# A hybrid attention/GLA/MoE layer on one core: the first two projections in quarters, shift and scale 256 columns at a time

## The reference

```
sh1, sc1, g1, sh2, sc2, g2 = split(SiLU(cond) @ w_ada + b_ada, 6)   # 1024 -> 6 x 1024
h = LN(x) * (1 + sc1) + sh1
q_a, k_a, v_a, q_g, k_g, v_g, r_g, lr, mg = split(h @ w_in)
```

## Time and profile before

| | |
|---|---|
| median of 3 runs | 675.63 us (674.58 to 676.66) |
| profiled execution: time, span | 672.36 us, 670.6 us |
| PE busy | 621.0 us, 93% |
| DVE, ACT, POOL busy | 40%, 16%, 17% |
| chain that ended last | PE 60%, DMA 22%, DVE 8% |

### The profile page before, as it was taken

One profiled execution on the slowest core, in us unless ns is written; L12 is line 12 of the kernel. 1 busy time (PEld: TensorE's weight loads), 2 busy tenths in 40 slices (PEclk: granted clock), 3 DMA queues, 4 the chain that ended last, 5 costly groups with the idle time before them and its releaser, 6 DMA issues.

```text
span 670.6 us, 8592 instructions
## 1 busy us (share of the span) xinstructions
PE 621.0 (93%) x3403; PEld 344.4 (51%) x3403; DVE 265.9 (40%) x593; ACT 106.6 (16%) x222; POOL 115.6 (17%) x114
## 2 busy tenths in 40 slices
PE   6999999999999999999999998999999887788994
PEld 3553355546455556555544464665566544444541
DVE  4322533145445544302224865334333232222347
ACT  2001553110032222330000021111111111111000
POOL 4000000010300000000001323334334222221102
PEclk9999999999999999999999999999999999988998
DMA  9998737344131130409995097899999999999862
GB/s 336 376 332 289 251 127 251 126 158 157 24 127 58 69 126 1 126 0 317 372 402 223 38 359 296 333 420 416 413 414 417 413 417 414 415 416 419 352 241 94
DMA packets 56200, 176.65 MB, mean 263 GB/s; under 512 B 10644, under 2 KB 12724, under 8 KB 44512
## 3 DMA queue, kind: packets, MB, share of 16 engines
q1 hardware_dynamic: 39264, 143.34, 55.4%
q10 hardware_dynamic: 11152, 24.47, 10.4%
q0 software_dynamic: 5744, 8.28, 3.5%
HBM read 174.58 MB, written 11.96 MB: 278 GB/s over the span
## 4 chain that ended last, share of the span: by engine, by line
PE 60%; DMA 22%; DVE 8%; issue 2%; POOL 2%; ACT 2%; SPq 2%; ACTq 0%; DVEq 0%; POOLq 0%
PE bank L1592 13%; PE bank L1865 11%; DMA X<-exp_w_up 8%; PE bank L1581 7%; PE bank L1766 6%; PE bank L1874 5%; DMA Y<-exp_w_up 4%; PE bank L1545 3%; DMA Y<-ln_b 3%; DMA X<-w_ada 2%; PE bank L1505 2%; DMA Y<-w_ada 2%; POOL rstd L689 2%; PE bank L1839 2%; PE bank L1733 1%
## 5 line engine op out<-in xcount | busy, mean ns | idle before, releaser
L1865 PE MATMUL bank<-X,Y 128*64 128x256 f32 x672 | 82.0, 395 | 11.8 <-DMA X<-exp_w_up 10.8
L1592 PE MATMUL bank<-Y,W 128*128 128x384 f32 x256 | 86.6, 492 | 0.0
L1865 PEld LDWEIGHTS bank<-X,Y 128*64 128x64 f32 x672 | 50.7, 137 | 48.0 <-DMA X<-exp_w_up 18.0
L689 POOL TENSOR_TENSOR rstd<-ss,cst 128x1 f32<-128x1 f32 (+3 forms) x21 | 22.6, 1075 | 295.7 <-DVE ss L822 295.7
L1592 PEld LDWEIGHTS bank<-Y,W 128*128 128x128 f32 x256 | 47.4, 190 | 36.0 <-issue 5.6
L1581 PE MATMUL bank<-W,Y 128*128 128x512 f32 x144 | 64.0, 597 | 0.0
L732 POOL DMA_INDIRECT Y<-h_rows,gidx x32 | 41.4, 1293 | 92.9 <-PE bank L1839 88.4
L1192 DVE COPY abias<-bank 128x128 f32<-128x128 f32 x32 | 9.3, 292 | 117.1 <-PE bank L1898 117.1
L1865 PE MATMUL bank<-W,Y 128*64 128x256 f32 (+1 forms) x320 | 37.2, 346 | 7.5 <-DMA W<-exp_w_up 3.9
L737 POOL DMA_INDIRECT pair_rows<-PTr,sidx x32 | 32.9, 1029 | 61.2 <-DVE PTr L1206 60.6
L1779 PE MATMUL bank<-X,Y 128*128 128x512 f32 x96 | 41.7, 594 | 1.3 <-issue 1.0
(11 more groups left out here) (232 smaller groups left out, 723.2 us busy)
## 6 DMA issues: line engine op xcount, KB each, us to landing
X<-exp_w_gate SPq DMA_DIRECT2D x22, 1024.0 KB, 22.1
X<-exp_w_up SPq DMA_DIRECT2D x22, 1024.0 KB, 26.1
X<-exp_w_down SPq DMA_DIRECT2D x22, 1024.0 KB, 26.6
Y<-w_ada ACTq DMA_DIRECT2D x16, 1024.0 KB, 8.2
W<-w_in SPq DMA_DIRECT2D x7, 2048.0 KB, 9.0
W<-exp_w_gate SPq DMA_DIRECT2D x10, 1024.0 KB, 22.1
W<-exp_w_up SPq DMA_DIRECT2D x5, 1024.0 KB, 26.7
W<-exp_w_down SPq DMA_DIRECT2D x5, 1024.0 KB, 29.7
```

Source lines behind the costliest of these rows:

```text
L689: nc.gpsimd.tensor_tensor(rstd[:, 0:n], ss[:, 0:n], const("mhalf", 0, n), ALU.pow)\
L1592: ins = mm(bank[:, 0:TOKENS], w[:, k, c * P:(c + 1) * P], hT[:, :, k, :], start=k == 0, stop=k == KT - 1)
L1865: ins = mm(bank[hh * 64:hh * 64 + 64, a:b], x_[:, c, h * 64:h * 64 + 64], rhs(hh), start=k == 0 and a == 0, stop=k == KT - 1, skip_group_c ...
```

## The change

The constants are loaded in two parts: `ident` and `selcol` first, the rest after the second quarter. The -0.5 that GpSimd takes a power with is a memset of its own. Shift and scale are computed in four steps of 256 columns each (`shift_scale(g)`: two loads of 1 MB, 32 matmul instructions, one add, one group of columns), and features are modulated and `kvl` and `gqk` contracted in four quarters of two k blocks. `w_ada` block 0 no longer passes through W. VectorE interleaves the statistics of one tile with the normalisation of another, and computes SiLU of cond after the first. Three quarters of both projections are issued before the loop; the last quarter is in it.

```diff
-CONSTS = dict(ident=P, incl_f=P, ...
+CONSTS = dict(ident=P, selcol=2, incl_f=P, ...
-FILL_START = 6
+FILL_START = 4
+FILL_QUARTER = 1
-            sp.dma_start(cst[:, :], T["consts"][:, 0:NCONST]).then_inc(S["consts_in"], 16)
+            sp.dma_start(cst[:, 0:early_consts], T["consts"][:, 0:early_consts]).then_inc(S["first_consts_in"], 16)
+            def load_shift_scale(g):
+                h = slice(QD * (g % 2), QD * (g % 2 + 1))
+                for n in (g // 2, 2 + g // 2):
+                    sp.dma_start(early[n][:, g % 2], wa[:, :, n * HALF + h.start:n * HALF + h.stop])\
+                        .then_inc(shift_scale_in[g], 16)
+            def load_quarter(g):
+                ks = slice(QK * g, QK * (g + 1))
+                for kind in QUARTERED:
...
+            for g in range(QUARTERS):
+                load_shift_scale(g)
+                load_quarter(g)
+                if g == 1:
+                    sp.dma_start(cst[:, early_consts:], T["consts"][:, early_consts:NCONST]).then_inc(S["consts_in"], 16)
+            small_loads()
...
+            first_norm_stats(0)
+            first_norm_stats(1)
+            first_norm(0)
+            silu_of_cond()
+            first_norm_stats(2)
+            first_norm(1)
+            first_norm(2)
+            for g in range(QUARTERS):
+                shift_scale(g)
+                modulate(g)
+            dve.wait_ge(S["consts_in"], 16)
...
-            for n in range(4):
-                bias_rows(n)
+            for g in range(QUARTERS):
+                quarter_bias_rows(g)
...
-            main.wait_full(act, "ada", 3)
+            main.wait_full(act, "shift_scale", QUARTERS - 1)
             for h in range(3):
                 ada_half(h)
...
+            def shift_scale(g):
+                pe.wait_ge(shift_scale_in[g], 32)
+                bank = main.claim(pe, "shift_scale", g)
+                for s in range(2):
+                    w = early[2 * s + g // 2][:, g % 2]
+                    for k in range(KT):
+                        j = k % 4
+                        ins = mm(bank[32 * j:32 * j + 32, s * QD:(s + 1) * QD], csil[:, k, :], w[:, k, :], start=k < 4,
+                                 stop=k >= 4, skip_group_check=True)
+                main.filled(ins, "shift_scale", g)
...
+            pe.wait_ge(S["first_consts_in"], 16)
             keep_busy(FILL_START)
             x_transposes(0)
             x_transposes(1)
             pe.wait_ge(S["cond_silu"], 2)
-            modulation(0)
+            shift_scale(0)
             x_transposes(2)
...
+            columns(0)
+            keep_busy(FILL_QUARTER)
+            for g in range(QUARTERS - 1):
+                for i in range(TILES):
+                    project_quarter("kvl", i, g)
+                project_quarter("gqk", 0, g)
+                shift_scale(g + 1)
+                project_quarter("gqk", 1, g)
+                columns(g + 1)
+                project_quarter("gqk", 2, g)
```

More of the change, by code:

```diff
@@ L95, in constants @@
     put("unused", np.repeat(EMPTY + (rows // SLOT_ROWS)[:, None], 2 * NE, 1))
-    put("mhalf", np.full((P, 8), -0.5))
     c[:, NCONST:] = 2 * np.arange(TOKENS)[None] + (rows // SLOT_ROWS)[:, None]
     return c
-WEIGHTS = ([("ada", 0)]
-           + [(x, 0) for x in ("kvl", "gqk", "vg", "q", "rg")] + [("mg", n) for n in range(4)]
+WEIGHTS = ([(x, 0) for x in ("kvl", "gqk", "vg", "q", "rg")] + [("mg", n) for n in range(4)]
            + [("br", n) for n in range(2)])
@@ L197, in wait_read @@
         eng.wait_ge(self.at[job][2], self.at[job][3] + 1)
-HALVED = ("kvl", "gqk")
+QUARTERED = ("kvl", "gqk")
+QUARTERS = 4
+QK = KT // QUARTERS
+QD = QK * P
 def first_jobs():
-    jobs = {("modc", g): 7 for g in range(2)}
+    jobs = {("modc", g): 7 for g in range(QUARTERS)}
     jobs.update({("xT", 0, 0): 0, ("xT", 0, 1): 1, ("xT", 1, 0): 3, ("xT", 1, 1): 0, ("xT", 2, 0): 1, ("xT", 2, 1): 3})
-    jobs.update({("ada", n): 2 for n in (0, 2, 1, 3, 4)})
-    for kind, ring in zip(HALVED, ((4, 5, 6), (3, 0, 1))):
+    jobs.update({("shift_scale", g): 2 for g in range(QUARTERS)})
+    jobs[("ada", 4)] = 2
+    for kind, ring in zip(QUARTERED, ((4, 5, 6), (3, 0, 1))):
         jobs.update({("proj", kind, 0, i): ring[i] for i in range(TILES)})
@@ L237, in main_jobs @@
     for j, x in enumerate(PROJ):
-        jobs += [("proj",) + x for _ in range(x[0] not in HALVED)] + [step for step in AFTER[j] if step[0] == "ada" and step[1] > 4]
+        jobs += [("proj",) + x for _ in range(x[0] not in QUARTERED)] + [step for step in AFTER[j] if step[0] == "ada" and step[1] > 4]
     jobs += [("br", c, m) for c in range(KT) for m in range(2)]
@@ L340, in program @@
         ada_ring = [y1[:, b * 4 * HALF:(b + 1) * 4 * HALF] for b in range(3)]
-        early = {2: X[:, 8544:8544 + KT * HALF], 1: X[:, 0:KT * HALF], 3: adabuf}
+        early = {0: X[:, 0:KT * HALF], 2: X[:, 8544:8544 + KT * HALF], 1: X[:, KT * HALF:2 * KT * HALF], 3: adabuf}
+        early = {n: a.rearrange("p (h k n) -> p h k n", h=2, k=KT) for n, a in early.items()}
         merged = lambda i: Y1[:, i, 0, :]
@@ L452, in program @@
         w_free = [sem(f"w_free{j}") for j in range(2)]
[L453 removed]
+        shift_scale_in = [sem(f"shift_scale_in{g}") for g in range(QUARTERS)]
         ada_in = [sem(f"ada_in{b}") for b in range(3)]
[L455 to L456 removed]
+        quarter_in = [sem(f"quarter_in{g}") for g in range(QUARTERS - 1)]
         wout_in = [sem(f"wout_in{j}") for j in range(2)]
@@ L578, in _ @@
                     sp.wait_ge(w_free[j % 2], j // 2)
[L579 to L592, removed]
+                if kind in QUARTERED:
+                    continue
+                if kind in ("vg", "q", "rg", "mg"):
                     c = {"vg": OFF[5], "q": 0, "rg": OFF[6], "mg": OFF[8] + n * HALF}[kind]
@@ L891, in modulation, with first_norm_stats, first_norm, silu_of_cond @@
                 main.was_read(ins, "ada", n)
[L894 to L902, removed]
-                dve.wait_ge(x_in[i], 16)
-                tell(norm(x[:, i, :], x[:, i, :]), "x_normed")
+            def first_norm_stats(i):
+                dve.wait_ge(x_in[i], 16)
+                half_stats(x[:, i, :], 0)
+                step(half_stats(x[:, i, :], 1))
+                step(V.bn_aggr(mv3[:, i, :], stats[:, 0:2, :].rearrange("p a b -> p (a b)")))
+                ask_power(ss[:, i:i + 1], mv3[:, i, 1:2], 1.0, EPS)
+            def first_norm(i):
+                dve.wait_ge(S["pow_done"], i + 1)
+                V.tensor_scalar(x[:, i, :], x[:, i, :], mv3[:, i, 0:1], rstd[:, i:i + 1], ALU.subtract, ALU.mult)\
+                    .then_inc(S["x_normed"], 1)
+            def silu_of_cond():
+                dve.wait_ge(S["cond_exp"], 1)
+                step(V.tensor_scalar_add(conde[:, :, :], conde[:, :, :], 1.0))
+                step(V.reciprocal(conde[:, :, :], conde[:, :, :]))
+                dve.wait_ge(S["zeros_set"], 5)
+                for s in range(2):
+                    ins = V.tensor_tensor(csil[:, :, s], cond[:, s, :], conde[:, s, :], ALU.mult)
+                    tell(ins, "cond_silu")
+            def shift_scale(g):
+                bank = main.wait_full(dve, "shift_scale", g)
+                bias, landed = quarter_bias(g)
+                dve.wait_ge(landed, 32)
+                ins = V.tensor_tensor(part[:, g, :], bank[:, :], bias, ALU.add)
+                main.was_read(ins, "shift_scale", g)
             def modulate(g):
@@ L1287, in _, with quarter_bias_rows @@
             act.wait_ge(S["zeros_set"], 5)
+            def quarter_bias_rows(g):
+                bias, landed = quarter_bias(g)
+                for s in range(2):
+                    act.dma_start(bias[0:2, s * QD:(s + 1) * QD],
+                                  T["b_ada"][0:1, s * D + g * QD:s * D + (g + 1) * QD].to_broadcast([2, QD]))\
+                        .then_inc(landed, 16)
             def bias_rows(n):
```

152 lines of the change are left out of this document (56 added, 96 removed).

## The result

The changed kernel takes 682.54 us in the median of 4 runs (678.74 to 684.02) against 675.14 for the kernel before, 7.4 us more; the ratio estimated from all runs of both is 1.0091, interval 1.0061 to 1.0121, which is 6.1 us (4.1 to 8.2). The forecast was 677.5, 1.9 us slower, range 673.3 to 680.7: the sign was right, the size three to four times too small, and the median lies outside. The profiled execution took 678.74 us (span 676.8), the fastest of the four; 6.2 us of span more than before.

The account below looks back on a forecast made before the run. Bound: a chain of waits through transfers and TensorE to modulation 5's end. `kvl` full 1.6 us later, modulation 4 1.8, modulation 5 1.9, carried to the end: 674.3 profiled, 677.5 us median, range 673.3 to 680.7.

Parts of the forecast that it names:

- The front: Start to first projection: shorter constants and smaller first loads let it start at about 19.0, 6.5 us earlier.
- A quarter: One of four steps of both projections: 11.1 us for the first, 10.97 for the next two; narrower `shift_scale` adds 0.05.
- `kvl` ends later though it begins earlier: First projection: full at 55.1 instead of 53.49, as `gqk` and modulation work moved in front of its end.
- Modulation 4: Queued behind `kvl`: ends at 57.55, 1.8 us later, including 0.2 us of wait for half 1 of the ring.
- Half 3: Ring load asked for after modulation 4: lands 9.6 us after issue, so modulation 5 ends at 68.25, 1.9 us later.
- The step that failed: TensorE at modulation 5: idles 4 us on half 3 instead of 0.64, with no slower work behind it in the sum.
- rival (a): Clock falls behind the half 3 wait (+2.1) or at the front (+2.5), or loads are slower: 679.5 to 680.5; chance 0.25.
- Rival (c): Two queues share evenly at half 3: it lands in 8.0 us, modulation 5 ends +0.3, 675.9; chance 0.15.
- (b): Half 3 lands in 5.5 to 5.6 us, TensorE doesn't idle, kernel 2.1 us faster, 673.5; chance 0.13.
- (d): Only the start counts: 6.5 us earlier with 2.6 more work behind, end moves by -3.9, 671.7; chance 0.04.
- Nothing is gained behind modulation 5: Before z(1): 1.8 us saved per `gqk` tile buys nothing, as z(1) still stands 4.2 us behind z(0).
- One shift carried to the end: From z(0) on: every later stage, loads included, shifts alike, +1.9 us in all.

Follow-up runs that it names:

- e8_two_fills: Changed kernel plus two fill matmuls between the transposes of tiles 0 and 1 and four at the wait for half 3; ratio 1.0045 to the kernel before.
- the second trace: Trace of the changed kernel run once more with nothing altered; ratio 1.0073 to the kernel before.

## Why the prediction was right or wrong

- **The front** (first projection at 19.0): right in the profiled execution, 19.08, and by luck: five of the six traces with this front and no fill in it have 19.9 to 20.7. "The fills end by 10 at the latest" and the stretch behind them were right as times, but I counted that stretch at the full clock. It is thin enough to lose it in most traces, which costs 1.2 us.
- **A quarter** (11.1, then 10.97 us; 256 columns cost 0.05 more): right, 11.0 measured; `shift_scale` takes 1.86 on the chain. Small rows did not hold TensorE: `shift_scale(0)` waited 0.2 us.
- **`kvl` ends later though it begins earlier** (55.1): right, 0.2 us later than I had it, and the central turn of the prediction.
- **Modulation 4** (57.55): it ended at 58.34. The wait on half 1 was 0.6 where I took 0.2, and `kvl` was 0.2 late.
- **Half 3** (9.6 us after its issue): 9.76 in one trace and about 11 in the other; why it was longer there is open. `vg` was asked for 3.0 us before it and not 2.2. Together with the line above the landing cost 2.9 us against 1.9. e8_two_fills, 3.0 us above the kernel before (1.8 to 4.3), bounds it from above, because it also has a slow `vg`.
- **The step that failed** is "so it idles 4 us on half 3 where it idled 0.64", costed as if the work behind it kept its speed. The idle was right (4.37), but the clock fell in it in both traces: 1.93 and 2.02 us of work on the chain instead of 1.07 and 1.06, 1.8 us that the sum put at nothing. I had this as rival (a), + 2.1, at 0.25, against it "seven gaps of about 2 us without a fall". But those idles were half as long, and one of the eight had lost the clock. No row was near 4 us, and seven short idles were no evidence on a long one. The rival's size for this, + 2.1, was near the measured 1.8. The same holds for the thin stretch at the front, which (a) also named and the sum put at nothing: it named 2.5 us, and the second trace shows 1.2. With 2.9 for the landing the three make 5.9, against 6.1 by the ratio; and the median lies above even the 680.5 of (a). The Trainium skill, "TensorE: Matmul & The Clock Gate", section "HAM oscillation", spoke against the forecast; by that rule the wait re-throttles TensorE, and the traces agree (granted clock 0.50 from 67 us).
- **Rival (c)**, even sharing of the two queues (8.0 us), is refuted: 9.76. Rivals (b) and (d) did not come.
- **Nothing is gained behind modulation 5**: right, z(1) stood 4.2 us behind the end of z(0), and the idle in front of it grew to 2.33 in the four quartered traces whose `gqk` tile there ran a single quarter at full clock and without a fill. That the clock falls behind this idle too, as it did in all four, I had not seen.
- **One shift carried to the end**: right to 414 us within 0.4. The remaining 1.6 us of the profiled execution, and the 3 to 5 by which the other three runs exceed it, are not settled. A fallen front clock, as in the second trace, would give 1.2 of them; the mean granted clocks of the three, 0.979 to 0.982 against 0.985, fit more slow work but don't say where. ScalarE's stop of 4.3 us at 422.8 is the only other place seen, in one trace, and no experiment touched it.

## What to carry to other kernels

An engine that starts earlier helps only if what it finishes first, and what others wait for, ends earlier too: here each quarter of two projections delayed the end of the first, and with it a buffer, a ring and a transfer. Before a wait is priced, look at how long the idle is and what the clock was behind the longest idles of the trace; a landing 2.9 us later cost 4.8 us here. And look at what time saved in one place leaves idle in another: the `gqk` work taken away in front of z(1) left 2.33 us, and the `vg` projection behind it slowed by 1.5 to 2.4. Where the rows show a chain that is a transfer, ask how far behind it the next one is: moving 16 us of transfer forward was worth 0.3, and 0.9 us gained at z(0) in the kernel before were gone at the next ring half.

## What had not been expected of the hardware

Around the transposes of two tiles, 1.1 us each, TensorE stood 0.5 to 1.1 us in front of the first and 2.2 in front of the second, and in five of six traces of the new front the granted clock then fell to between 0.50 and 0.55. In the sixth the first idle was 0.42 and the clock stayed at 1.00. A fill of 1.9 us between them kept it at 1.00 in the traces of all four kernels that had it.

Idles of 1.6 to 2.1 us left the clock up in front of seven of eight expert groups of the kernel before, while 2.33 us in front of z(1) lost it in four traces of four. The eighth group lost it behind 2.02 us where another kept it behind 2.09, and at the front 2.17 us went either way. So the length of that one idle did not decide it.

The same load, half 3, took 9.5 us beside another of 2 MB in the kernel before and 9.8 and 11 in the two traces of the changed one, and 5.9 when the other was held back.
